# An eight-core retention, attention and expert kernel: only the gate/up expert weights converted ahead, the value products one step later, the attention accumulators copied out

## What is computed

```python
# layer 0: retention, then a dense channel mixer, then the shared K and V
x = x + retention_mixer(rms_norm(x, ln_mix[0]), ret_w_in, ret_w_o)      # 4 heads, qk 256, v 512
x = x + swiglu(rms_norm(x, ln_ffn[0]), ffn_w_gu, ffn_w_down)            # 2816 wide
k_sh, v_sh = shared_kv(x, kv_norm, w_kv, cos, sin)
# layer 1: differential attention, block-causal mask, then 2 of 8 experts
sc = einsum('bhcqd,bhckd->bhcqk', q_blk, k_sh) * scale
p = softmax(where(mask, sc, neg))
a = p[:, :, 0] - lam * p[:, :, 1]
o = einsum('bhqk,bhkv->bhqv', a, v_sh)                                  # 8 heads, v 128
for e in range(N_EXPERTS):                                              # 8 experts, 3584 wide
    y = y + gates[:, e:e+1] * ((silu(t @ w_g[e]) * (t @ w_u[e])) @ w_down[e])
```

## Time and profile before

| | |
|---|---|
| runs, us | 6006.25, 6025.62, 6653.9; median 6025.62 |
| the profiled execution | 6063.09 us, slowest core (2) 6061.5 us |
| the other cores' spans | 5960.5 to 6027.0 us |
| TensorE busy | 4876.3 us, 80% of the span |
| VectorE, ScalarE, GpSimd busy | 1763.9, 1776.7, 1058.2 us |
| granted TensorE clock, mean | 0.893 |
| DMA | 1012.79 MB written by the queues, 44.8% of 16 engines' span on the software queue (GpSimd's), 21.2% on the hardware queue (SyncE's) |

### The profile page before, as it was taken

The page is one execution under the profiler, slowest core; times in us unless marked ns, Lnnn a source line. Parts: engine busy times, 40 slices in busy tenths (PEclk is TensorE's granted clock), DMA queues, the critical chain, the costliest instruction groups (busy, mean ns, idle before and its releaser), DMA issues.

```text
span 6061.5 us, 82130 instructions; the slowest of 8 cores (5960.5 to 6061.5 us)
## 1 busy us (share of the span) xinstructions
PE 4876.3 (80%) x28514; PEld 2497.1 (41%) x28514; DVE 1763.9 (29%) x4466; ACT 1776.7 (29%) x2695; POOL 1058.2 (17%) x1302
## 2 busy tenths in 40 slices
PE   5787788886778889998674747465999999999991
PEld 2343333442334344443342424232456455556540
DVE  3444444443122222222432323134111111111114
ACT  2333333332122222222463636452121111111111
POOL 2332223232000000000110101012122122122113
PEclk9898999997889999999876767677999999999996
DMA  8955554555976666665499999914576466466546
GB/s 170 206 160 166 175 159 141 166 169 139 169 155 159 149 142 153 154 156 138 130 110 121 115 121 115 129 54 161 193 259 231 179 246 243 174 244 247 191 160 232
DMA packets 242595, 1012.79 MB, mean 167 GB/s; under 512 B 89360, under 2 KB 102160, under 8 KB 165904
## 3 DMA queue, kind: packets, MB, share of 16 engines
q0 software_dynamic: 73696, 594.73, 44.8%
q1 hardware_dynamic: 168496, 412.81, 21.2%
HBM read 1104.07 MB, written 298.32 MB: 231 GB/s over the span
## 4 chain that ended last, share of the span: by engine, by line
PE 67%; DMA 9%; DVE 7%; another core or an unknown queue 6%; issue 5%; ACT 3%; POOL 2%; DVEq 0%; SPq 0%; POOLq 0%; ACTq 0%
PE p_pp L1364 19%; PE p_pp L1381 9%; PE p_pp L749 8%; PE p_pp L544 7%; PE p_pp L1024 5%; PE p_pp L845 4%; PE p_pp L619 3%; DMA kTs<-s_kst 3%; PE p_pp L768 3%; PE p_pp L1000 2%; PE p_pp L506 2%; DMA s_wr<-lwb 2%; PE p_pp L391 1%; DMA s_xf<-xms 1%
## 5 line engine op out<-in xcount | busy, mean ns | idle before, releaser
L1364 PE MATMUL p_pp<-s_hT,s_wbC 128*128 128x512 bf16 (+1 forms) x4672 | 790.7, 331 | 5.1 <-issue 3.7
L1024 PE MATMUL p_pp<-s_VX,s_ex 128*128 128x129 bf16 x4352 | 421.3, 246 | 384.1 <-DMA s_VX<-vs 181.1
L1010 ACT ACTIVATE s_ex<-p_pp 128x1024 bf16<-128x1024 f32 (+3 forms) x640 | 537.0, 924 | 476.5 <-PE p_pp L1000 473.1
L749 PE MATMUL p_pp<-s_hF,s_gw 128*128 128x512 bf16 x2816 | 647.7, 386 | 1.3 <-ACT s_hF L393 1.3
L1364 PEld LDWEIGHTS p_pp<-s_hT,s_wbC 128*128 128x128 bf16 x4672 | 457.0, 98 | 327.3 <-issue 10.8
L1024 PEld LDWEIGHTS p_pp<-s_VX,s_ex 128*128 128x128 bf16 x4352 | 295.0, 108 | 557.8 <-issue 554.8
L1369 DVE TENSOR_TENSOR s_big<-p_pp,s_sgc 128x512 bf16<-128x512 f32 (+1 forms) x420 | 237.6, 567 | 919.2 <-PE p_pp L1364 844.0
L544 PE MATMUL p_pp<-s_wr,s_hTr 128*128 128x512 bf16 x2048 | 492.5, 396 | 0.0
L1367 ACT ACTIVATE s_sgc<-p_pp 128x512 bf16<-128x512 f32 (+1 forms) x420 | 208.2, 497 | 914.0 <-PE p_pp L1364 858.6
L749 PEld LDWEIGHTS p_pp<-s_hF,s_gw 128*128 128x128 bf16 x2816 | 276.4, 99 | 325.4 <-issue 22.3
L1381 PE MATMUL p_pp<-s_wbC,s_big 128*128 128x512 bf16 x1776 | 395.4, 379 | 0.0
(11 more groups left out here) (225 smaller groups left out, 5437.1 us busy)
## 6 DMA issues: line engine op xcount, KB each, us to landing
mwb<-moe_w POOLq DMA_DIRECT2D x168, 1024.0 KB, 33.1
s_wr<-lwb SPq DMA_DIRECT2D x112, 1024.0 KB, 12.1
s_wf<-lwb SPq DMA_DIRECT2D x56, 1024.0 KB, 6.5
ys<-s_yst SPq DMA_DIRECT2D x46, 512.0 KB, 2.8
s_wr<-lw POOLq DMA_DIRECT2D x16, 1024.0 KB, 21.3
s_xn<-x SPq DMA_DIRECT2D x32, 512.0 KB, 10.3
lwb<-s_wr SPq DMA_DIRECT2D x16, 1024.0 KB, 21.8
s_xr<-x SPq DMA_DIRECT2D x64, 256.0 KB, 10.6
```

Source lines behind the costliest of these rows:

```text
L749: k.op("pe", lambda e, kc=kc: e.matmul(P, lhsT=wb[:, kc * 512 + c0:kc * 512 + c0 + 128], rhs=hT1[:, kc, :], start=(kc == 0), stop=(kc == 7 ...
L1010: k.op("act", lambda e: e.activation(out=e_[:, :, lo:512], in_=SP2[n % 2][:].rearrange("p (c t) -> p c t", c=2)[:, :, lo:512], func=AF.Exp ...
L1024: k.op("pe", lambda e, c=c, jj=jj, j=j: e.matmul(PO[jj][:, c * 129:(c + 1) * 129], lhsT=e_[:, c, jj * 128:(jj + 1) * 128], rhs=VX[h % 2][: ...
L1364: k.op("pe", lambda e, kc=kc, P=P, c0=c0: e.matmul(P[:, 0:n], lhsT=wb[:, kc * 512 + c0:kc * 512 + c0 + 128], rhs=hTp[:, kc, 0:n], start=(k ...
```

## The change

Six edits:

1. `mwb` holds gate/up tiles alone, 112 instead of 168. In the expert passes the down tiles are gathered from the float32 tensor `moe_w`, converted on the way into SBUF. The row numbers `wix` are therefore made in two parts.
2. `convert` writes its DMA over rows of 1024 columns (`rearrange("r (a c) -> r a c", c=1024)`).
3. The places of the conversions: retention two in each of the items 4 to 29 (52 in all); dense one in steps 1 and 4 of the down projection of the tiles 0 to 6 (14); attention one in 12 steps (46).
4. In `kv_units` four staging tiles `kst` instead of two.
5. In attention the value products of step n-2 are issued in step n, and the first key block of a group goes over the accumulators from 0 to 3 instead of 3 to 0.
6. `att_out` first copies the accumulator to SBUF (`pcp`, 128 x 258, float32) and reads the copy.

Besides, DMA semaphores are used again after a barrier (`free`, `mark`); the program needs 66 of them instead of 147.

```diff
@@ -339,8 +353,10 @@
         def convert(n):
             for _ in range(n):
                 i = conv_no[0]
-                if i < NEXP * NCH:
-                    k.dma("pool", mwb[i * 128:(i + 1) * 128, :], moe_w[i * 128:(i + 1) * 128, :], wr=[R_mwb], disjoint=True)
+                if i < NEXP * NGU:
+                    r0 = (i // NGU * NCH + i % NGU) * 128
+                    k.dma("pool", mwb[i * 128:(i + 1) * 128, :].rearrange("r (a c) -> r a c", c=1024),
+                          moe_w[r0:r0 + 128, :].rearrange("r (a c) -> r a c", c=1024), wr=[R_mwb], disjoint=True)
                     conv_no[0] += 1
 
 
@@ -648,8 +665,8 @@
                         load_xn(t + 1, 1)
                     if hd == 3 and t + 1 < NT:
                         load_cs(t + 1)
-                    if i + 2 < len(items):
-                        convert(1)
+                    if i >= 4 and i + 2 < len(items):
+                        convert(2)
                     for b in range(4):
                         if hd == 2 and t + 1 < NT:
                             norm0_front(t + 1, b)
@@ -761,7 +778,7 @@
                             if b == 0:
                                 stt["w"] = rg.next(T_KV + nci)
                             wb, R_w = stt["w"]
-                            pr = stt["n"] % 2
+                            pr, ps_ = stt["n"] % 2, stt["n"] % 4
                             stt["n"] += 1
                             P, _, R_P = bank()
                             for kc in range(8):
@@ -820,8 +837,6 @@
                             kv.pop(0)()
                         if fc == 10:
                             load_xt(t)
-                        if fc % 3 == 2 and fc < 18:
-                            convert(1)
                     assert not kv
                     k.dma("sp", dcsT[:], dcs[t * 512:(t + 1) * 512, :].rearrange("(b p) d -> p b d", p=128), wr=[R_dcsT])
                     more = t + 1 < NT
@@ -848,6 +863,8 @@
                                          rd=[R_w, R_actT[fc]], wr=[R_P])
                             if more and step < 4:
                                 norm1_back(step)
+                            if more and step in (1, 4):
+                                convert(1)
                         for b in range(4):
                             P, bi, R_P = acc[b]
                             held.discard(bi)
@@ -899,6 +916,7 @@
                 osb2 = [k.sb("osb%d" % i, [128, 128], F32, pes) for i in range(4)]; R_osb2 = [Reg() for _ in range(4)]
                 tcb2 = [k.sb("tcb%d" % i, [128, 128], F32, pes) for i in range(4)]; R_tcb2 = [Reg() for _ in range(4)]
                 asm = [k.sb("asm%d" % i, [128, 8], F32, pes) for i in range(4)]; R_asm = [Reg() for _ in range(4)]
+                pcp = [k.sb("pcp%d" % i, [128, 258], F32, pes) for i in range(4)]; R_pcp = [Reg() for _ in range(4)]
                 print("SBUF left, attention", nc.sbuf_bytes_remaining)
 
                 def get_x(j):
@@ -1018,7 +1036,7 @@
                     h, g, kb = steps[n]
                     lo = span_of(n)
                     e_, R_e = ex[n % NE], R_ex[n % NE]
-                    for jj in range(3, lo // 128 - 1, -1):
+                    for jj in (range(4) if kb == 0 else range(3, lo // 128 - 1, -1)):
                         j = 4 * g + jj
                         for c in range(2):
                             k.op("pe", lambda e, c=c, jj=jj, j=j: e.matmul(PO[jj][:, c * 129:(c + 1) * 129],
@@ -1030,8 +1048,9 @@
 
                 def att_out(h, g, jj):
                     j = 4 * g + jj
-                    P, R_P = PO[jj], R_PO[jj]
                     s_, R_s = asm[jj], R_asm[jj]
+                    P, R_P = pcp[jj][:], R_pcp[jj]
+                    k.op("dve", lambda e: e.tensor_copy(out=P, in_=PO[jj][:, 0:258]), rd=[R_PO[jj]], wr=[R_P])
                     k.op("dve", lambda e: e.reciprocal(out=s_[:, 0:2], in_=P[:, 0:258].rearrange("p (c d) -> p c d", c=2)[:, :, 128]),
                          rd=[R_P], wr=[R_s])
                     k.op("dve", lambda e: e.tensor_tensor(out=s_[:, 2:3], in0=s_[:, 1:2], in1=NEGLAM, op=ALU.mult), rd=[R_s, R_NEGLAM], wr=[R_s])
@@ -1058,13 +1077,14 @@
                     att_exp(n)
                     if pend_ao:
                         pend_ao.pop(0)()
-                    if n > 0:
-                        att_pv(n - 1)
+                    if n > 1:
+                        att_pv(n - 2)
                     if g == 0 and kb == 2 and h + 1 < 8:
                         load_head(h + 1)
-                    if n % 6 == 3:
+                    if n % 12 == 3:
                         convert(1)
-                assert conv_no[0] == NEXP * NCH
+                assert conv_no[0] == NEXP * NGU
+                att_pv(len(steps) - 2)
                 att_pv(len(steps) - 1)
                 for f in pend_ao:
                     f()
@@ -1136,7 +1157,10 @@
                         if NB - 4 <= i < NB:
                             for z in range(4):
                                 k._deps("pool", (), [R_ao[4 * (i - NB + 4) + z]])
-                        k.gather(ring[i % NB], mwb[:, :], wix[:, passes[p][0], c:c + 1], rd=[R_wix, R_mwb], wr=[R_ring[i % NB]])
+                        if c < NGU:
+                            k.gather(ring[i % NB], mwb[:, :], wix[:, passes[p][0], c:c + 1], rd=[R_wix[0], R_mwb], wr=[R_ring[i % NB]])
+                        else:
+                            k.gather(ring[i % NB], moe_w[:, :], wix[:, passes[p][0], c:c + 1], rd=[R_wix[1]], wr=[R_ring[i % NB]])
                         wst["issued"] += 1
 
                 def next_w(p, c):
@@ -1278,11 +1302,13 @@
                 dv(lambda e: e.tensor_tensor(out=e8[:, 1, 0:7], in0=cinc[:, 1, :].unsqueeze(1).to_broadcast([128, 7, 8]),
                                              in1=b3(rcst[:, 24:31], 7), op=ALU.is_le), [R_cinc, R_rcst], [R_e8])
                 dv(lambda e: e.reduce_sum(out=exs[:], in_=e8[:].rearrange("p z a b -> p (z a) b")[:, 0:NPASS, :], axis=AX), [R_e8], [R_exs])
-                dv(lambda e: e.tensor_scalar(out=exs[:], in0=exs[:], scalar1=float(NEXP - 1), scalar2=float(NCH * 128), op0=ALU.min, op1=ALU.mult),
-                   [R_exs], [R_exs])
-                dv(lambda e: e.tensor_tensor(out=wix[:], in0=exs[:].unsqueeze(2).to_broadcast([128, NPASS, NCH]),
-                                             in1=rcst[:, 32:32 + NCH].unsqueeze(1).to_broadcast([128, NPASS, NCH]), op=ALU.add),
-                   [R_exs, R_rcst], [R_wix])
+                for z, (lo, hi, n) in enumerate(((0, NGU, NGU), (NGU, NCH, NCH))):
+                    dv(lambda e, z=z, n=n: e.tensor_scalar(out=exm[z][:], in0=exs[:], scalar1=float(NEXP - 1), scalar2=float(n * 128),
+                                                           op0=ALU.min, op1=ALU.mult), [R_exs], [R_exm[z]])
+                    dv(lambda e, z=z, lo=lo, hi=hi: e.tensor_tensor(
+                        out=wix[:, :, lo:hi], in0=exm[z][:].unsqueeze(2).to_broadcast([128, NPASS, hi - lo]),
+                        in1=rcst[:, 32 + lo:32 + hi].unsqueeze(1).to_broadcast([128, NPASS, hi - lo]), op=ALU.add),
+                       [R_exm[z], R_rcst], [R_wix[z]])
                 issue_w(4)
                 dv(lambda e: e.tensor_tensor(out=cexc, in0=cinc, in1=big_sm, op=ALU.subtract), [R_cinc, R_big_sm], [R_cexc])
                 dv(lambda e: e.tensor_scalar(out=c1, in0=cexc[:, 0, :], scalar1=float(TS), scalar2=None, op0=ALU.mult), [R_cexc], [R_c1])
```

30 lines of the change are left out of this document (22 added, 8 removed).

## The result

The changed kernel takes 5834.19 us (median; 5826.64 to 5851.0). Beside it the kernel before took 6006.25 and 6025.62 us (two more runs of it, in which one die was at a lower clock, are left out), and the ratio is 0.970, with an interval of 0.966 to 0.975: 3.0% faster. The prediction was 5794, 3.9% less, with a range of 5690 to 5925. The profiled execution took 5835.35 us, its slowest core (1) 5833.8; the others 5698.6 to 5818.1.

What follows compares the result with a forecast made beforehand. TensorE was 80% busy, three of its waits caused by conversions' 32 KB DMA packets. Terms: 6063 + 53 - 179 - 186 + 0 + 80 = 5831 us, on the median 5794, range 5690 to 5925.

Steps and rivals of the forecast that it cites:

- The pieces: Conversions written over 1024-column rows: folded back, so packets stay 32 KB at 7.6 to 9.5 us a conversion; term 0.
- Retention: Retention's weight loads: a second conversion delays each of seven late loads by 7.6 us; +53 us, bounds +30 to +75.
- Dense: Dense: K-store waits (-141) and first down weights (-37) end, clock -11, late ring loads +10; -179 us, bounds -190 and -150.
- Attention, the load: Attention's `VX` loads: fewer conversions end the waits, -181 us and -5 of half clock; bounds -190 and -150.
- the steps: Attention's masked steps: VectorE sets the pace whatever TensorE's distance; copy +14 and sooner free accumulators -14; 0 us.
- Experts: Two-block expert passes: float32 down tiles at 6.24 us, TensorE stands 9.9 us, 11.4 with half clock; seven passes, +80 us.
- The sum: Whole kernel, on the profiled execution: 6063 + 53 - 179 - 186 + 0 + 80 = 5831 us, 232 less.
- The median: Whole kernel, on the median of the runs: 6026 - 232 = 5794 us, -3.9%.
- (a): Expert passes become bound by DMA: at 9.5 us a tile +239 us, result 5953; chance 0.15 for 9.5 or more.
- (b): Attention's steps gain: mask waits go and the clock stays up; -137 us more, 5657 us; chance 0.1.
- (c): Conversions come in small packets on the chip, so retention's loads are not delayed; 5657 us; chance 0.05.
- (d): `kTs` and `VX` waits move instead of going; half of 322 us stays, 5955 us; chance 0.05.

Runs made afterwards that it cites:

- the second trace of these instructions: Kernel before with only the seven expert down tiles gathered from float32 `moe_w`, all 168 conversions kept, unchanged up to the experts; span 6085.2 us.

## Why the prediction was right, and where it was not

The conversions, the late loads and the price in the expert passes came as forecast. Two steps failed: the last one, which took the saving read in one long execution from the median, and the claim on the masked steps. By its own steps, each term beside what it measured:

- *The pieces*, 0: right. The packets are of 32 KB. What was wrong is the sentence beside it that with 4 KB packets other places would gain little and the stalls would be an eighth. In the trace of small packets (2 KB) `VX` doesn't wait and the K turns cost 29 us, more than an eighth of the 83 to 141 that they were; but GpSimd stood up to 51 us at an issue, and nothing was won.
- *Retention*, +53: +55. Seven waits, 127.7 us where 135 were named (8.4 to 25.2 us each, not 15 to 24), and 8.0 us for a second load. Moving the 14 conversions shows the cause: issued right behind a load, they delay it.
- *Dense*, -179: -188 in this pair of executions, with the K waits and the first down weights gone as said, and 3.5 us of ring waits in place of 10. Either cure alone does nearly do: fewer conversions in other places ended all K waits with two tiles, four staging tiles alone all but those of one tile.
- *Attention, the load*, -186, and *the steps*, 0: together -194. `VX` doesn't wait at all. The stage came to 822 us, below the 835 to 850 named as a sign, in part since the 1025 us that it was reckoned from held some 8 us of other work. The 0 was right as a sum only (+3), by luck: two errors cancelled. The step that failed is that the masked steps cost 13.1 us "whatever TensorE's distance". Distance and order alone cut the mask waits from 139 to 85 us and the stage by 23, where I had given 14 for accumulators that come free sooner; and the copy cost 26, not 14. The price of the pair, 3.73, was met (3.74).
- *Experts*, +80: +99 on the slowest core, with 80.7 us of waits in the seven passes of two blocks where 7 x 9.9 = 69 were reckoned, none in those of four, and 6.2 us a tile where 6.24 was taken. The half clock behind the waits was under-sized: 1.5 us a pass, while PE's busy time for the same products grew by 27 us, 3.8 a pass. (The two come to 8 us more than the stage grew; 6 us of short idle times that the stage had before are gone.) By the Trainium skill ("DMA: Bandwidth & Descriptors", Where 436 GB/s comes from), with 358 GB/s for a core, our estimate was 5.9 us a tile and a term of 63. The trace, with 6.2 us, is nearer to the row taken.
- *The sum* on the profiled execution: -232 against -228, 5831 against 5835.35 us. That it is this near is partly luck: dense and attention gave 17 us more than said, the experts cost 19 us more.
- *The median*: this is the step that put the forecast 40 us too low: "On the median: 6026 - 232 = 5794". What was won there is 6026 - 5834 = 192 us (182 from the mean of 6006.25 and 6025.62). The terms were read on the slowest core of an execution 37 us above the median, and the one that doesn't carry over is dense, -179. Its K waits of 140.7 us were 110.9 and 100.1 on cores 0 and 1 of the same execution, and 83 to 90 in the second trace of these instructions, where the slower core of each pair had dense in 1343 to 1350 instead of 1401 us. From there to the changed kernel's 1213 it is some 130 to 137 us and not 188. The executions that make the median were not traced; but their times, and the 5991 to 6006 us beside the experiments, say that the profiled one was unusual. A saving read in a long execution has to be taken from that execution's time (5831), not from the median. Why its stores to `kTs` came later stays open.
- *The rivals*: none came. (a) the price was 6.2 and not 9.5 us; (b) the mask waits stayed at 138 us in the changed kernel, though only because the copy gave back what the distance had won; moving the chains brought what (b) had promised, -148; (c) packets stayed large; (d) the K and `VX` waits went and did not move.
